# Four blocks of modulation rows beside the choice of keys, taken by GpSimd and a column of ones

## The chip, the cores and the metric

One NeuronCore of one Trainium2 chip runs the whole program in one launch. The metric is the device time of that launch in microseconds, lower is better. In the profile PE is TensorE's matmul, PEld its weight loads, DVE VectorE, ACT ScalarE, POOL GpSimd and SP the engine that issues the weight DMAs.

## The reference, cut to what matters

Three model blocks run one after the other over one sequence of 512 tokens with 1024 features, all in float32. The change lies in the first. There a modulation vector is made from a condition vector, two branches (RWKV and sparse attention) run on the same activations, and the branches are merged with sigmoid gates:

```python
mod = jax.nn.silu(c) @ w_ada + b_ada
shift, scale, gate = jnp.split(mod, 3, axis=-1)
h = rms_norm(x, norm_w) * (1.0 + scale[:, None, :]) + shift[:, None, :]
p = h @ w_in
...
idx_score = jnp.einsum('bqhs,bqh->bqs', jax.nn.relu(sc), iwb)
idx_score = jnp.where(adm[None], idx_score, -jnp.inf)
_, sel = lax.top_k(idx_score, topk)
...
yb = (yb * jax.nn.silu(gb)) @ w_b_out
merged = jax.nn.sigmoid(gm_a) * ya + jax.nn.sigmoid(gm_b) * yb
```

`top_k` takes 128 keys for each query: this is the choice of keys. The second model block has a modulation vector of its own (`w_mod`), which is needed only once the second block begins; its products with `silu(c_2)` are spread over the first block. A modulation vector is a product of one row (or of two, where a second condition is needed) with a 1024 x 512 weight block, so almost no arithmetic on 2 MB of weights.

## The kernel before

**Weights.** Weights are streamed from HBM in blocks of 2 MB (1024 rows by 512 columns, laid as 128 partitions by 8 by 512). In this part of the program they go into a ring of four slots, `weight_ring`. The order of the blocks is written out in `block1_plan`; `Chip.stream` (L223 to L265) issues them in that order from SP's queue, and before each issue SP waits until the last reader of the slot's former block has signalled (`free_at`). A block thus waits for the block four places ahead of it.

**Stages.** `project` (L493 on) runs one stage: a list of tiles in the order in which TensorE computes them. Each tile is (block, kind, place, source, tokens, evictions). A tile of kind "T" is 8 accumulated matmuls of 128x128 weights on 128x512 activations; one of kind "M" is a modulation tile; one of kind "X" is a transpose. ScalarE (first entry of the evictions) or VectorE (second) takes each finished tile out of PSUM. In this stage four PSUM banks are used in turn (`banks=4`), so that a tile waits for the eviction of the tile four places ahead. With `tensor_beside`, `scalar_beside` and `vector_beside` at -1, further work stands on an engine ahead of the tiles; `vector_after` stands behind them on VectorE.

**The stage of the change** is the sixth `project` of `block1`. It has seven blocks. Block 0 holds the gate columns of the attention branch (four tiles, `gates`), blocks 1 and 4 the sigmoid gates of the merge (four tiles each), blocks 2 and 3 the last two blocks of `w_ada`, and blocks 5 and 6 two blocks of `w_mod`. The stage's engines do this:

- TensorE first computes the 24 index dots of `dsa_scores` (L2130), three query groups of eight heads. ScalarE takes each through a ReLU (L2140) and VectorE multiplies it by its weight and adds it to the score (L2150 for the first head of a group, L2152 for the other seven, two inputs in SBUF). Four banks and four rooms lie between them: dot i waits for ReLU i-4, ReLU i waits for addition i-4.
- Then TensorE goes through the tiles, and VectorE, which evicts nothing here, makes the choice of keys, `dsa_select`: for each of three query groups an addition of the mask (L2170), 16 rounds of the eight largest (L2172) and their replacement (L2173), and the bias (L2174).
- An "M" tile (L617 to L620) loads the conditions `csil` (128 x 32) as weights and moves the weight block through the array in 32 matmuls of 128 columns. ScalarE copies the rows to `mstage` (L743); an "X" tile transposes them back to columns with one matmul (L592), and ScalarE adds the bias and writes `mod1` or `mod2` in four small operations (L736, `turn_beside_choice`).

The next stage is the attention (`dsa_attention`), whose first operation on VectorE (L2028) reads the bias that the choice of keys wrote. GpSimd has no work in this stage, nor anywhere ahead of the end of the second model block.

Of the kernel before, what the change touches and what calls it, by code (L numbers as in the profile page):

```python
# [16 lines left out]
ACT = mybir.ActivationFunctionType  # L17
AXX = mybir.AxisListType.X
MUL, ADD, SUB, MAX, MIN = ALU.mult, ALU.add, ALU.subtract, ALU.max, ALU.min

P = 128
T = 512
D = 1024
KD = D // P
# [467 lines left out]

def project(ch, nblocks, tiles, ahead=None, extra_sync=None, vector_first=None, vector_after=None, scalar_after=None,  # L493
            banks=BANKS, tensor_beside={}, vector_beside={}, scalar_beside={}, norm=None, normed_from=0, order=None, split=None,
            joined=None, early=None):

# [40 lines left out]
    with nullcontext(ch.block) as block:  # L539
        @block.sync  # L540
        def _(sp):
# [2 lines left out]
                extra_sync(sp)  # L544
            ch.stream(sp, first + nblocks + ahead)

        @block.tensor
        def _(pe):
            last = -1
            if joined:  # L550
                pe.wait_ge(by_act.sem, by_act.at(0))
                pe.wait_ge(by_dve.sem, by_dve.at(0))
            meet(pe)
            tensor_beside.get(-1, nothing)(pe)
            if split:
                count, half_ready, between = split
                ch.block_wait(pe, first)
                half_ready(pe)
                for n in range(count):
                    _, _, where, src, ntok, _ = tiles[n]  # L560
                    for k in range(2):
                        pe.matmul(ch.ps[:, order[n], 0:ntok], ch.block_view(first)[:, k, where:where + P], src[:, k, 0:ntok],
                                  start=k == 0, stop=False)
                    between.get(n, nothing)(pe)
            if early:
                count, half_ready, between = early
                for n in range(count):
                    b, _, where, src, ntok, _ = tiles[n]
                    ch.block_wait(pe, first + b)
                    for k in range(4):  # L570
                        half_ready(pe, k)
                        if k:
                            between.get(n - 1 + k / 4, nothing)(pe)
                        pe.matmul(ch.ps[:, order[n], 0:ntok], ch.block_view(first + b)[:, k, where:where + P], src[:, k, 0:ntok],
                                  start=k == 0, stop=False)
                    between.get(n, nothing)(pe)
            for n, t in enumerate(tiles):
                b, kind, where, src, ntok, ev = t
                i = first + b if b is not None else None
                if b is not None and b != last:  # L580
                    ch.block_wait(pe, i)
                    last = b
                if n >= R:
                    if tiles[n - R][5][1] is not None:
                        pe.wait_ge(by_dve.sem, by_dve.at(int(nv[n - R])))
                    else:
                        pe.wait_ge(by_act.sem, by_act.at(int(na[n - R])))
                m, f = shape(t)
                bank = ch.ps[:, order[n % R], :]
                if kind == "X":  # L590
                    pe.wait_ge(by_act.sem, by_act.at(int(na[where])))
                    ins = pe.transpose(bank[:, 0:P], src, ch.m("ident"))  # L592
                    ins.then_inc(ready.sem, 1)
                    ready.total += 1
                    tensor_beside.get(n, nothing)(pe)
                    continue
                w = ch.block_view(i)
                _, kt, c = ch.plan[i]
                if kind[0] == "W":
                    a_, b_, need_w, need_h = product_operands(ch, i, kind[1], src)  # L600
                    if need_w:
                        pe.wait_ge(weight_ready.sem, 4 * ch.sum_order[i] + need_w)
                    if (norm or src is not None) and need_h:
                        pe.wait_ge(h_ready.sem, h_ready.at(need_h))
                    for j in range(2):
                        if j == 1 and n - 0.5 in tensor_beside:
                            tensor_beside[n - 0.5](pe)
                        for k in range(4):
                            if n == normed_from and j == 0 and norm:
                                norm.wait(pe, k)  # L610
                            if n == normed_from + 1 and j == 0 and norm and kind[1] == 2:
                                norm.wait(pe, 4 + k)
                            cols = slice(j * P, (j + 1) * P)
                            st, mv = (b_[:, k, cols], a_[:, k, :]) if kind[2] else (a_[:, k, cols], b_[:, k, :])
                            ins = pe.matmul(bank[:, j * L:(j + 1) * L], st, mv, start=k == 0, stop=k == 3)  # L615
                elif kind == "M":
                    for k in range(kt):  # L617
                        for g in range(4):
                            ins = pe.matmul(bank[32 * g:32 * g + 32, 0:P], ch.csil[:, k, :],  # L619
                                            w[:, k, g * P:(g + 1) * P], start=k == 0, stop=k == kt - 1)  # L620
                else:
                    for k in range(2 if split and n < split[0] else 4 if early and n < early[0] else 0, kt):
                        if early and n == 0:
                            early[1](pe, k)
                        if n == normed_from and norm:
                            norm.wait(pe, k)
                        if k and n - 1 + k / kt in tensor_beside:
                            tensor_beside[n - 1 + k / kt](pe)
                        if kind == "T":
                            ins = pe.matmul(bank[0:m, 0:f], w[:, k, where:where + m], src[:, k, 0:ntok],  # L630
                                            start=k == 0, stop=k == kt - 1)
                        else:
                            c0 = kind[1] if isinstance(kind, tuple) else 0
                            ins = pe.matmul(bank[0:m, 0:f], src[:, k, where:where + P], w[:, k, c0:c0 + f],  # L634
                                            start=k == 0, stop=k == kt - 1)
                ins.then_inc(ready.sem, 1)
                ready.total += 1
                tensor_beside.get(n, nothing)(pe)
# [87 lines left out]
    return out + [turn_rows(ch, bands[x[0]], *x) for x in pending], len(place)  # L726


def turn_beside_choice(ch, band, i, m):

    dst, bias, first = band
    n = dst.shape[2]

    def part(a, act, ps, sig):
        for g in range(4):
            a(act.activation(dst[:, g, :], ps[:, 32 * g + first:32 * g + first + n], ACT.Identity, bias=bias[:, g:g + 1]),  # L736
              sig if g == 3 else None)
    return (None, "X", m, ch.mstage[:, i, :], T, (part, None))


def copy_to(out):

    return (lambda a, act, ps, sig: a(act.copy(out, ps), sig), None)  # L743


def act_to(out, func, **kw):
    return (lambda a, act, ps, sig: a(act.activation(out, ps, func, **kw), sig), None)
# [1451 lines left out]
def block1(ch):  # L2199
# [7 lines left out]

    gate, ga = ch.slot(3), ch.slot(5, 2)
    gates = [(0, "T", j * P, ch.hT, T, act_to(gate[:, j, :], ACT.Silu)) for j in range(4)]
    tiles = [(b, "T", j * P, ch.hT, T, act_to(ga[:, 4 * i + j, :], ACT.Sigmoid)) for i, b in enumerate((1, 4)) for j in range(4)]  # L2210
    bands = gate_bands(ch) + bands2(ch, 10, 12)
    rows = [(b, "M", 0, None, T, copy_to(ch.mstage[:, i, :])) for i, b in enumerate((2, 3, 5, 6))]
    turns = [turn_beside_choice(ch, band, i, m) for i, (band, m) in enumerate(zip(bands, (8, 9, 13, 15)))]
    tiles = (gates + tiles[0:4] + rows[0:2] + turns[0:1] + tiles[4:5] + turns[1:2] + rows[2:3] + tiles[5:6] + rows[3:4]
             + turns[2:3] + tiles[6:7] + turns[3:4] + tiles[7:8])
    project(ch, 7, tiles, banks=4, tensor_beside={-1: score_tensor}, scalar_beside={-1: score_scalar},
            vector_beside={-1: score_vector}, vector_after=dsa_select(ch))

    merged, gb, y, yb, tmp = ga, ch.slot(0, 2), ch.slot(2), ch.slot(11), ch.slot(9)
    tiles = []  # L2220
# [63 lines left out]
def block1_plan(A):  # L2284
# [4 lines left out]
    return ([ada[0], ada[1], lora, k, ada[2], ada[3], r, m[0], m[1], v, m[2], g, m[3], m[4], None, None]  # L2289
            + blocks(w, 3200, 3712) + blocks(w, 2176, 2688) + [None, None] + blocks(w, 2688, 3200)  # L2290
            + weave(blocks(w, 4224, 4736) + joined(w, [(4736, 4808)]), m[5:10]) + blocks(w, 3712, 4224)
            + blocks(w, 4808, 5320) + ada[4:6] + blocks(w, 5320, 5832) + m[10:12] + blocks(A["w_a_out"], 0, 1024)
            + blocks(w, 5832, 6856) + blocks(A["w_b_out"], 0, 1024)
            + blocks(A["w_o"], 0, 1024))

# [1511 lines left out]
```

## Time and profile before

| | us |
|---|---|
| median of 3 runs | 3161.09 |
| lowest and highest | 3160.84, 3163.19 |
| the profiled execution | 3161.36 |
| span of that execution in the trace | 3159.4 |

Of the span PE is busy 3015.5 us, VectorE 1552.0 us, ScalarE 700.8 us and GpSimd 9.6 us. The stage of the change starts at about 434.7 us of the span, with the index dots, and its last tile is evicted at 538.6 us.

How to read it: the rows below come from one profiled execution, and times in them count from the start of its span. In a timeline row the first number is the start, the second how long the stretch lasts; "xN" behind it is how many instructions of the same kind are merged in it, and the bracket holds idle time ahead of it and who ended it. One float32 matmul of the program is two matmul records in the trace, each with its own weight load; a transpose is one.

### The profile page before, as it was taken

How to read it: one execution, taken by the hardware profiler on the slowest of the kernel's cores; microseconds unless marked ns; L12 is line 12 of the kernel's file. 1: busy time of each engine (PE TensorE's matmuls, PEld its weight loads, DVE VectorE, ACT ScalarE, POOL GpSimd, SP SyncE). 2: the span in 40 equal slices, each digit the busy share in tenths (PEclk: the TensorE clock that was granted, in tenths of full speed). 3: DMA queues.
4: the chain of work that ended last, by engine and by line, in shares of the span. 5: the costliest groups of instructions: out<-in, count | busy, mean ns of one | idle time of the engine just before them, and what ended most of it. 6: DMA issues, size and time to landing. Idle time of an engine off the chain costs nothing.

```text
span 3159.4 us, 41395 instructions
## 1 busy us (share of the span) xinstructions
PE 3015.5 (95%) x17400; PEld 1797.4 (57%) x17400; DVE 1552.0 (49%) x2453; ACT 700.8 (22%) x1192; POOL 9.6 (0%) x10
## 2 busy tenths in 40 slices
PE   9999999999999899999899898999999999999998
PEld 4485544676457333332232233787588887887875
DVE  4463375655967322211211212545586857576663
ACT  4110332413063100000000001010632333331413
POOL 0000000000000000000000001000000000000000
PEclk9999999999999999999999999999999999999999
DMA  7301254031223899999999999131111211221210
GB/s 288 133 3 55 84 187 158 29 120 64 80 76 129 358 427 428 428 427 427 428 427 428 427 428 378 67 113 65 61 67 58 76 67 68 81 80 54 81 54 27
DMA packets 115575, 587.61 MB, mean 186 GB/s; under 512 B 6976, under 2 KB 8256, under 8 KB 89664
## 3 DMA queue, kind: packets, MB, share of 16 engines
q1 hardware_dynamic: 115392, 584.98, 46.2%
q8 instruction: 138, 2.26, 0.3%
q14 instruction: 45, 0.37, 0.0%
HBM read 582.86 MB, written 2.10 MB: 185 GB/s over the span
## 4 chain that ended last, share of the span: by engine, by line
PE 75%; DMA 15%; DVE 6%; issue 1%; SPq 1%; ACT 1%; DVEq 0%; ACTq 0%
PE ps L615 25%; PE ps L630 21%; DMA work<-in_w_up 7%; PE ps L2822 6%; DMA weight_ring<-in_w_up 5%; PE ps L2903 4%; PE ps L634 2%; PE ps L2785 2%; PE ps L1446 2%; DMA spare_slot<-in_w_up 1%; SPq L262 1%; PE ps L3535 1%; PE ps L3498 1%; PE ps L619 1%; DMA spare_slot<-in_first_weights 1%
## 5 line engine op out<-in xcount | busy, mean ns | idle before, releaser
L630 PE MATMUL ps<-hT,weight_ring 128*128 128x512 f32 (+1 forms) x1016 | 444.9, 594 | 1.4 <-ACT work L743 1.2
L630 PEld LDWEIGHTS ps<-hT,weight_ring 128*128 128x128 f32 (+1 forms) x1016 | 190.0, 190 | 233.3 <-issue 229.3
L399 DVE TENSOR_TENSOR work<-work,ps 128x512 f32<-128x512 f32 x203 | 139.5, 687 | 247.6 <-PE ps L615 243.5
L615 PE MATMUL ps<-weight_ring 128*128 128x256 f32 x992 | 225.6, 380 | 0.0
L2822 PE MATMUL ps<-work 128*64 128x512 f32 x832 | 191.0, 602 | 24.9 <-DMA work<-in_w_up 17.6
L630 PE MATMUL ps<-work,weight_ring 128*128 128x512 f32 (+1 forms) x496 | 210.6, 571 | 0.0
L2987 DVE SCALAR_TENSOR_TENSOR xT<-ps,mod,xT 128x512 f32<-128x512 f32 x128 | 96.1, 751 | 230.5 <-PE ps L2836 220.7
L2822 PE MATMUL ps<-weight_ring,work 128*64 128x512 f32 x800 | 181.7, 598 | 22.0 <-DMA weight_ring<-in_w_up 13.2
L615 PEld LDWEIGHTS ps<-weight_ring 128*128 128x128 f32 x992 | 187.1, 190 | 25.1
L615 PE MATMUL ps<-weight_ring,spare_slot 128*128 128x256 f32 x800 | 181.6, 380 | 0.0
L615 PE MATMUL ps<-hT,weight_ring 128*128 128x256 f32 x736 | 168.6, 386 | 6.3 <-DVE hT L850 3.8
L615 PEld LDWEIGHTS ps<-weight_ring,spare_slot 128*128 128x128 f32 x800 | 151.3, 190 | 20.8 <-issue 0.7
L615 PEld LDWEIGHTS ps<-hT,weight_ring 128*128 128x128 f32 x736 | 140.6, 193 | 27.9 <-issue 6.4
L2934 ACT ACTIVATE work<-ps 128x512 f32<-128x512 f32 x32 | 34.2, 1070 | 500.9 <-PE ps L2822 500.4
L2822 PEld LDWEIGHTS ps<-work 128*64 128x64 f32 x832 | 57.7, 137 | 150.8 <-issue 111.6
L630 PEld LDWEIGHTS ps<-work,weight_ring 128*128 128x128 f32 x496 | 90.8, 190 | 88.5 <-issue 84.4
L2822 PEld LDWEIGHTS ps<-weight_ring,work 128*64 128x64 f32 x800 | 55.3, 136 | 141.7 <-issue 107.3
L2981 DVE TENSOR_TENSOR work<-work,ps 128x512 f32<-128x512 f32 x32 | 33.9, 1058 | 188.8 <-PE ps L2822 188.3
L615 PE MATMUL ps<-work,weight_ring 128*128 128x256 f32 x448 | 100.9, 380 | 4.5 <-issue 4.5
L615 PEld LDWEIGHTS ps<-work,weight_ring 128*128 128x128 f32 x448 | 84.5, 190 | 16.8 <-issue 5.8
L2315 DVE SCALAR_TENSOR_TENSOR work<-work,vectors 128x512 f32<-128x512 f32 x120 | 90.2, 752 | 4.3
L2975 DVE TENSOR_TENSOR work<-ps,small 128x512 f32<-128x512 f32 (+1 forms) x17 | 11.2, 660 | 160.0 <-PE ps L2794 159.9
(490 smaller groups left out, 4150.0 us busy)
## 6 DMA issues: line engine op xcount, KB each, us to landing
work<-in_w_up SPq DMA_DIRECT2D x27, 2048.0 KB, 42.5
weight_ring<-in_w_gate SPq DMA_DIRECT2D x26, 2048.0 KB, 45.2
work<-in_w_gate SPq DMA_DIRECT2D x25, 2048.0 KB, 45.2
weight_ring<-in_w_down SPq DMA_DIRECT2D x24, 2048.0 KB, 44.5
weight_ring<-in_w_up SPq DMA_DIRECT2D x24, 2048.0 KB, 42.3
work<-in_w_down SPq DMA_DIRECT2D x24, 2048.0 KB, 44.9
weight_ring<-in_w_in_odd SPq DMA_DIRECT2D x20, 2048.0 KB, 7.7
weight_ring<-in_w_in SPq DMA_DIRECT2D x15, 2048.0 KB, 8.7
```

Of the source, the lines that this page charges most:

```text
L399: v(dve.tensor_tensor(out, x, got, op), sig if out is steps[-1][0] else None)
L615: ins = pe.matmul(bank[:, j * L:(j + 1) * L], st, mv, start=k == 0, stop=k == 3)
L630: ins = pe.matmul(bank[0:m, 0:f], w[:, k, where:where + m], src[:, k, 0:ntok], start=k == 0, stop=k == kt - 1)
L634: ins = pe.matmul(bank[0:m, 0:f], src[:, k, where:where + P], w[:, k, c0:c0 + f], start=k == 0, stop=k == kt - 1)
L1446: ins = pe.matmul(ps[rows, bank, cols], mat(left, par, q, s), moving, start=True, stop=True)
L2315: v(dve.scalar_tensor_tensor(y[:, j, :], src, tap, y[:, j, :], MUL, ADD), tapped if w == 30 else None)
L2785: ins = pe.matmul(ps[64 * q:64 * q + 64, bank, c], oh[:, s, :], hN[:, s, q * 512 + c.start:q * 512 + c.stop], start=s == 0, stop=s == 3)
L2822: ins = pe.matmul(ps[64 * h:64 * h + 64, 1 + 2 * u + n, :], xs[:, 2 * (i % 2) + t, i // 2, :], w[:, t, c0:c0 + 512], start=i == 0 and t == ...
L2903: ins = pe.matmul(ps[64 * q:64 * q + 64, 7, :], hidT[:, i // 2, t, i % 2, :], w[:, t, q * 512:(q + 1) * 512], start=i == 0 and t == 0, sto ...
L2934: a(act.activation(by_tile(hid[:, p, :]), strided(ps[:, 1 + p, :]), ACT.Silu), silus)
L2981: v(dve.tensor_tensor(by_tile(hid[:, p, :]), by_tile(hid[:, p, :]), strided(ps[:, 3 + p, :]), MUL), hid_ready)
L2987: v(dve.scalar_tensor_tensor(ch.xT[:, n, :], ps[:, scatter_banks(e, i // 2)[i % 2], :], ch.mod2[:, 40 + n, 0:1], ch.xT[:, n, :], MUL, ADD) ...
```

## The change

The modulation work of the four blocks moves from TensorE to GpSimd. For each of the four blocks GpSimd waits until it has arrived, multiplies it in place by the condition (`csil`, one column of the wanted condition, spread over 512), and adds its eight 512-wide pieces in three halving steps, the last into a room in work slot 1. It waits for each of its own four steps before the next, and counts them on `pool_step`. A new tile kind "C" has TensorE multiply the room with a column of ones: four matmuls of 128x128 weights on a 128x1 column, which sum over the partitions and leave 128 columns of modulation in one PSUM column each. The "M" tiles, the copies to `mstage` and the "X" tiles of this stage go. ScalarE's four small operations stay, on one column instead of one or two (the second condition's gate is not read).

The blocks of the stage stand in a new order in `block1_plan`: the `w_ada` blocks are now blocks 1 and 2, the first merge block is block 3, the `w_mod` blocks are 4 and 5, the second merge block is 6. A block that GpSimd reads is given back to SP by GpSimd's fourth step on it.

```diff
@@ project
-            joined=None, early=None):
+            joined=None, early=None, pool=None):
...
+        if pool:
+            block.gpsimd(pool)
...
+                if kind == "C":
+                    pe.wait_ge(*where)
+                    for g in range(4):
+                        ins = pe.matmul(bank[:, g:g + 1], src[:, g * P:(g + 1) * P], ch.m("ones")[:, 0:1], start=True, stop=True)
+                    ins.then_inc(ready.sem, 1)
+                    ready.total += 1
+                    tensor_beside.get(n, nothing)(pe)
+                    continue
...
-def turn_beside_choice(ch, band, i, m):
...
+def rows_on_pool(ch, first, rows):
+
+    rooms = ch.slot(1)
+    step = ch.counter("pool_step")
+    there = [(step.sem, step.at(4 * i + 4)) for i in range(len(rows))]
+    for i, (b, _) in enumerate(rows):
+        ch.free_at[first + b] = there[i]
+
+    def pool_rows(pool):
+        line = Line(pool, step)
+        ch.meet(pool)
+        for i, (b, (_, _, column)) in enumerate(rows):
+            ch.block_wait(pool, first + b)
+            w, acc = ch.block_view(first + b), rooms[:, i, :]
+            line(pool.tensor_tensor(w, w, ch.csil[:, :, column:column + 1].to_broadcast([P, KD, T]), MUL))
+            line(pool.tensor_tensor(w[:, 0:4, :], w[:, 0:4, :], w[:, 4:8, :], ADD))
+            line(pool.tensor_tensor(w[:, 0:2, :], w[:, 0:2, :], w[:, 2:4, :], ADD))
+            line(pool.tensor_tensor(acc, w[:, 0, :], w[:, 1, :], ADD))
+
+    def taken(i):
+        dst, bias, _ = rows[i][1]
+
+        def part(a, act, ps, sig):
+            for g in range(4):
+                a(act.activation(dst[:, g, 0:1], ps[:, g:g + 1], ACT.Identity, bias=bias[:, g:g + 1]), sig if g == 3 else None)
+        return (None, "C", there[i], rooms[:, i, :], T, (part, None))
+    return pool_rows, [taken(i) for i in range(len(rows))]
@@ block1
-    tiles = [(b, "T", j * P, ch.hT, T, act_to(ga[:, 4 * i + j, :], ACT.Sigmoid)) for i, b in enumerate((1, 4)) for j in range(4)]
+    tiles = [(b, "T", j * P, ch.hT, T, act_to(ga[:, 4 * i + j, :], ACT.Sigmoid)) for i, b in enumerate((3, 6)) for j in range(4)]
     bands = gate_bands(ch) + bands2(ch, 10, 12)
-    rows = [(b, "M", 0, None, T, copy_to(ch.mstage[:, i, :])) for i, b in enumerate((2, 3, 5, 6))]
-    turns = [turn_beside_choice(ch, band, i, m) for i, (band, m) in enumerate(zip(bands, (8, 9, 13, 15)))]
-    tiles = (gates + tiles[0:4] + rows[0:2] + turns[0:1] + tiles[4:5] + turns[1:2] + rows[2:3] + tiles[5:6] + rows[3:4]
-             + turns[2:3] + tiles[6:7] + turns[3:4] + tiles[7:8])
+    pool_rows, turns = rows_on_pool(ch, ch.used, list(zip((1, 2, 4, 5), bands)))
+    tiles = gates + tiles[0:3] + turns[0:2] + tiles[3:6] + turns[2:3] + tiles[6:7] + turns[3:4] + tiles[7:8]
     project(ch, 7, tiles, banks=4, tensor_beside={-1: score_tensor}, scalar_beside={-1: score_scalar},
-            vector_beside={-1: score_vector}, vector_after=dsa_select(ch))
+            vector_beside={-1: score_vector}, vector_after=dsa_select(ch), pool=pool_rows)
@@ block1_plan
-            + blocks(w, 4808, 5320) + ada[4:6] + blocks(w, 5320, 5832) + m[10:12] + blocks(A["w_a_out"], 0, 1024)
+            + ada[4:6] + blocks(w, 4808, 5320) + m[10:12] + blocks(w, 5320, 5832) + blocks(A["w_a_out"], 0, 1024)
```

TensorE's order in this stage before the change, from the index dots to the stage's end (numbers are the shape of the moving operand and how many instructions stand in a row):

```order
L2130 MATMUL ps<-work 128x512 x8
L630 MATMUL ps<-hT,weight_ring 128x512 x64
L619 MATMUL ps<-weight_ring,silu_of_conditions 32x128 x64
L592 MATMUL ps<-masks,modulation_rows 128x128
L630 MATMUL ps<-hT,weight_ring 128x512 x8
L592 MATMUL ps<-masks,modulation_rows 128x128
L619 MATMUL ps<-weight_ring,silu_of_conditions 32x128 x32
L630 MATMUL ps<-hT,weight_ring 128x512 x8
L619 MATMUL ps<-weight_ring,silu_of_conditions 32x128 x32
L592 MATMUL ps<-masks,modulation_rows 128x128
```

And the same place after the change, to the stage's end, where L641 is the old L630 and L596 the new tile:

```order
L2158 MATMUL ps<-work 128x512 x8
L641 MATMUL ps<-hT,weight_ring 128x512 x56
L596 MATMUL ps<-masks,work 128x1 x8
L641 MATMUL ps<-hT,weight_ring 128x512 x24
L596 MATMUL ps<-masks,work 128x1 x4
L641 MATMUL ps<-hT,weight_ring 128x512 x8
L596 MATMUL ps<-masks,work 128x1 x4
L641 MATMUL ps<-hT,weight_ring 128x512 x8
```

The 128 modulation matmuls and four transposes are gone, and 16 matmuls on one column stand behind the 7th, 10th and 11th of the 12 big tiles.

SP's queue at the same place before the change; the last three blocks ahead of the branch row are blocks 1 to 3 of the stage, and block 0 is the other one of the `x2`:

```order
L264 DMA weight_ring<-in_w_mod 128x8x512 x4
L264 DMA weight_ring<-in_w_in 128x8x512 x2
L264 DMA weight_ring<-in_w_ada 128x8x512 x2
L540 UNCONDITIONAL_BRANCH
L264 DMA weight_ring<-in_w_in 128x8x512
L264 DMA weight_ring<-in_w_mod 128x8x512 x2
L264 DMA weight_ring<-in_w_a_out 128x4x512 x2
```

SP's queue there after the change:

```order
L264 DMA weight_ring<-in_w_mod 128x8x512 x4
L264 DMA weight_ring<-in_w_in 128x8x512
L264 DMA weight_ring<-in_w_ada 128x8x512 x2
L264 DMA weight_ring<-in_w_in 128x8x512
L540 UNCONDITIONAL_BRANCH
L264 DMA weight_ring<-in_w_mod 128x8x512 x2
L264 DMA weight_ring<-in_w_in 128x8x512
L264 DMA weight_ring<-in_w_a_out 128x4x512 x2
```

The `w_ada` blocks moved one place forward, and the second merge block went from ahead of the two `w_mod` blocks to behind them; the amount of data is the same.

## Rows read from the trace of the kernel before

**Rows 1.** The page: busy time of each engine; granted PE clock in 40 slices.

```profile
PE 3015.5 (95%) x17400; PEld 1797.4 (57%) x17400; DVE 1552.0 (49%) x2453; ACT 700.8 (22%) x1192; POOL 9.6 (0%) x10
...
PEclk9999999999999999999999999999999999999999
```

**Rows 2.** The chain that ended last, 430 to 545 us: start, us, what.

```profile
435.97 11.00 PE ps L2130 x35
446.97 55.13 PE ps L630 x128
502.11 3.63 PE ps L619 x128
505.74 0.26 PE ps L592
505.99 6.87 PE ps L630 x16
512.97 1.88 PE ps L619 x64
...
531.04 6.88 PE ps L630 x16
538.01 0.61 ACT work L747
538.66 0.49 PE ps L1969 x4
```

**Rows 3.** Timeline of DVE, end of the choice and start of the attention.

```profile
513.15 0.43 DVE L2174 TENSOR_SCALAR work<-work 128x512 f32<-128x512 f32 x1
539.34 0.29 DVE L2028 CUSTOM_DVE_ANT_0 work<-ps,work 128x128 f32<-128x128 f32 x1 [25.77 <-PE ps L1969]
```

**Rows 4.** L2634 and L2649: records, ns min/median/max, first and last start in us.

```profile
L2634 PE MATMUL ps<-masks,work x8: 262/262/263, 1023.5 to 1024.3; 128*128 128x16 f32 x8
...
L2649 PE MATMUL ps<-small,masks x32: 200/201/228, 1028.0 to 1029.2; 128*32 128x4 f32 x32
```

**Rows 5.** Timeline of SP's queue, 426 to 429 us, and DMAs issued there with us to landing.

```profile
426.97 0.89 SPq L264 DMA_DIRECT2D weight_ring<-in_w_in  x1
...
weight_ring<-in_w_in SPq DMA_DIRECT2D x1, 2048.0 KB, 15.3
```

**Rows 6.** The same two views, 429 to 431 us and 474 to 475.5 us.

```profile
weight_ring<-in_w_ada SPq DMA_DIRECT2D x1, 2048.0 KB, 18.0
...
474.73 0.37 SPq L264 DMA_DIRECT2D weight_ring<-in_w_in  x1
...
weight_ring<-in_w_in SPq DMA_DIRECT2D x1, 2048.0 KB, 7.6
```

**Rows 7.** Groups by line and form: GpSimd's one operation, and VectorE's two-input sums.

```profile
L3018 POOL TENSOR_SCALAR work<-xT,small 128x512 f32<-128x512 f32 x6 | 9.4, 1582 | 1957.2 <-DVE xT L2987 1957.2
...
L3591 DVE TENSOR_TENSOR work<-work 128x2048 f32<-128x2048 f32 x8 | 18.3, 2292 | 0.3
...
L3464 DVE TENSOR_TENSOR work<-work 128x512 f32<-128x512 f32 x32 | 22.1, 691 | 1.1
```

**Rows 8.** Timeline of DVE, 436 to 452 us: the score additions.

```profile
440.54 4.54 DVE L2152 SCALAR_TENSOR_TENSOR work<-work,small 128x384 f32<-128x384 f32 x7
445.12 0.49 DVE L2150 TENSOR_SCALAR work<-work,small 128x512 f32<-128x512 f32 x1
445.64 5.48 DVE L2152 SCALAR_TENSOR_TENSOR work<-work,small 128x512 f32<-128x512 f32 x7
```

**Rows 9.** GpSimd and VectorE side by side: L3018 and L3010, ns min/median/max; timeline at 1965 us.

```profile
L3018 POOL TENSOR_SCALAR work<-xT,small x6: 1562/1563/1677, 1957.3 to 1965.3; 128x512 f32<-128x512 f32 x6
...
L3010 DVE TENSOR_SCALAR work<-xT,small x2: 486/596/706, 1966.1 to 1966.6; 128x512 f32<-128x512 f32 x2
...
1965.35 1.68 POOL L3018 TENSOR_SCALAR work<-xT,small 128x512 f32<-128x512 f32 x1
1966.08 0.49 DVE L3010 TENSOR_SCALAR work<-xT,small 128x512 f32<-128x512 f32 x1
```

More of the change, by code:

```diff
@@ L726, in modulated @@
     return out + [turn_rows(ch, bands[x[0]], *x) for x in pending], len(place)
-def turn_beside_choice(ch, band, i, m):
[L731 to L738, printed above, removed]
+def rows_on_pool(ch, first, rows):
[21 more added lines that the diff above has]
+    return pool_rows, [taken(i) for i in range(len(rows))]
 def copy_to(out):
```

## The prediction

> **What bounds the kernel now.** I read the page's busy line first, then the chain that ended last, cut to this stage, then VectorE's timeline, to see whether TensorE or the choice of keys ends the stage. PE is busy 95% of the span at a full granted clock [rows 1]: the level of 2.4 GHz, with no fall near this stage. In the chain the stage is TensorE from the index dots to the last tile: 11.0 us of dots to 446.97, eight big tiles in 55.13 us (6.89 each), then modulation and four more tiles to 538.01, where ScalarE's last eviction hands over to the attention at 538.66 [rows 2]. VectorE ends the choice at 513.58 and does nothing until 539.34, when it waits for TensorE [rows 3]. So TensorE's time is the stage's time, the choice has 25.8 us to spare, and GpSimd is empty. A saving here is not given back later for any reason that I see: the later transfers are issued when TensorE frees their slots, and shift with it.
>
> **What TensorE loses.** From 502.11 to 538.01 there are 35.90 us, in which four big tiles take 6.87 to 6.88 each, 27.5 in all [rows 2]. The rest, 8.4 us, is modulation: two blocks at once cost 3.63, the other two 1.88 each (one of them in the rows), 7.4 together, and about 1.0 is four transposes and the gaps at their ends. All of it lies on the path. Taken away: **-8.4**.
>
> **What TensorE gains.** Sixteen matmuls of full 128x128 weights on one column are 32 records. The nearest row has the same weights on 16 columns: eight records start between 1023.5 and 1024.3, seven steps of 0.114 us [rows 4]. The weight load sets this pace and doesn't shrink with the column, so 32 x 0.114 = 3.65 us. Bounds: records with 32 weight columns start 31 steps in 1.2 us, 0.039 each, giving 1.2 us; with nothing overlapped the record's own 262 ns would give 8.4 us [rows 4]. I take 3.65, since weights and shape are the same there. In the old order a tile behind a modulation block cost up to 0.2 us more, so three places add about 0.3. **+3.95**. The net is -4.45, and the tiles would end at 533.6 if TensorE waits for nothing.
>
> **ScalarE** loses four copies and keeps its sixteen small operations. It was waiting for TensorE; nothing on the path. The banks are no tighter: two C tiles in a row need banks whose tiles were evicted long before.
>
> **When GpSimd can start.** The first `w_ada` block takes the place in SP's queue that the merge block had: issued at 426.97, landed 15.3 us later, at 442.3 [rows 5]. The second one takes the next place, issued at 429.68 and landed 18.0 later, at 447.7 [rows 6]. Its other wait, for the engines of the stage before, ends ahead of that, near 434.6. The merge block now comes third, near 452, and is wanted only behind four tiles at 474.5. The first `w_mod` block waits for block 0's last tile as the merge block did: issued at 474.73, landed 482.3 [rows 6]. The second is issued at once behind it if GpSimd is done with block 1, and lands near 488.
>
> **How fast GpSimd is.** It does 4096 + 2048 + 1024 + 512 = 7680 columns for a block. The trace has it only in L3018, one input, 512 columns in 1562 ns: 3.05 ns a column [rows 7, 9], so 23.4 us a block. The lower bound is VectorE with two inputs, 2292 ns for 2048 or 1.12 a column, 8.6 us a block [rows 7]. Part of L3018 is the start of an instruction: VectorE's two-input sum falls from 1.35 ns a column at 512 to 1.12 at 2048, a factor of 0.83 [rows 7]. The same factor on 3.05 gives 2.53 ns and **19.4 us a block**, which I take: it is the row of this engine, corrected for length. That a second input costs more isn't in any row; it is in the range. The Trainium skill, "GPSIMD Engine Reference", section "Performance versus the Vector engine", has 4497 ns for a two-input float32 sum of 2048 columns, which by estimate would make about 17 us a block and change nothing below.
>
> **What waits for GpSimd.** TensorE is queued in order, so each C tile that comes too early holds every tile behind it. Times in the new order: tiles 1 to 7 end at 495.2, then blocks 1 and 2 are wanted, and come at 442.3 + 38.8 = 481. The second merge block needs the slot of block 2: issued at 481, landed about 489 to 494, wanted at 504 behind one more tile. Block 4 is wanted at 517.8: it starts at 482.3 (landing) and is done by 502. Block 5 is wanted at 525.7 and done at 521. Nothing waits, but the last C tile has only 4 us of slack. The general rule: with T us a block, block 5 is done at 442.3 + 4T, so **T = 21** (2.7 ns a column) is the point from which TensorE waits, and each us of T more costs 4.
>
> **VectorE beside GpSimd.** From 442.3 on GpSimd reads SBUF beside the score additions. The only overlap in the trace: the first L3010 ran from 1966.08 in 486 ns wholly inside a GpSimd operation that lasted to 1967.03 and wasn't slowed, the second took 706, and GpSimd's own 1677 instead of 1562 [rows 9]. So a slowing of up to 1.45, and no standstill. The additions that TensorE's last dot hangs on are those of the 384-wide group; they end at 445.08, and the last four start after 442.3, 0.65 us each [rows 8]. At 1.45 that is 4 x 0.29 = **+1.1** on TensorE (bounds: 0 from the unslowed one, and the standstill below). The eight 512-wide additions and the small operations of the choice may be slowed too, but have the 25.8 us to hide in; the rounds of L2172 and L2173 read one tensor.
>
> **Sum.** Against the profiled execution: 3161.4 - 8.4 + 3.95 + 1.1 = 3158.0. The profiled execution is 0.3 above the median, which is well within its error: I forecast **3158.0**.
>
> **Rival 1, GpSimd as slow as its row.** At 23.4 us a block, block 5 is done at 442.3 + 93.7 = 536.0. TensorE waits from 526.8 to 536.0 and ends at 536.0 + 1.0 + 6.9 = 543.9, 5.9 later than now: **3167**. For it: it is the only row of this engine, and has one input where the change has two. Against: the length of the instructions. It decides from 21 us a block, breaks even at 22.
>
> **Rival 2, a standstill.** If a two-input VectorE operation had to wait for the whole of a GpSimd instruction that is under way, the last four 384-wide additions would each sit out one of the four steps of block 1 (19.4 us together), then the next four ones those of block 2. TensorE's dots end 19.4 later and the tiles at 553. The choice starts 39 later and meets the steps of blocks 4 and 5 at its mask additions and bias operations, some 11 more, to end at 564; the attention then starts about 25 late instead of TensorE's 15. That is 3176 to 3187, say **3182**, slower. Against it speaks the unslowed L3010 inside L3018 [rows 9], which has one tensor input; for it, that no row has two inputs beside GpSimd. The Trainium skill, "SBUF — State Buffer", section "Who interferes with whom", states just this: a shared port pair as an exclusive lock for a whole instruction, taken also by a VectorE operation with two SBUF inputs. By the row on L3010 the trace doesn't agree for one input; for two it is silent.
>
> **Rival 3, it moves nothing.** If the small matmuls cost their full 262 ns a record, the 8.4 us come back whole: **3161.5**. The steps of 0.114 speak against it.
>
> **How the numbers follow.** A measurement of this kernel can tell about 0.2% from no change, 6.3 us, so 3154.8 to 3167.4 is "same". The forecast with its own range 3155.5 to 3160.5: 0.60. Rival 1: 0.16, over 3160 to 3172, half of it inside "same". Rival 2: 0.16. Rival 3: 0.08. The saving can pass 6.3 only if the column matmuls run at 0.039 a record (8.4 - 1.2 - 0.3 = 6.9 without contention): 0.05 of the first case. Faster 0.05, same 0.55 + 0.08 + 0.08 = 0.71, slower 0.08 + 0.16 = 0.24. The range 3155 to 3170 holds the forecast's case, rival 3 and most of rival 1, 0.80.
>
> **What would show it.** No L619 and L592 in this stage, and 32 records of L596 in about 3.7 us. GpSimd's four steps of a block at about 10.4, 5.2, 2.6 and 1.3 us; the last block's end before TensorE wants it, and L596 with no idle time ahead of it. The 384-wide additions at up to 0.9 us instead of 0.65, and the first big tile at 447 to 448.5. If a two-input addition shows 5 to 10 us, rival 2 holds; if L596 waits for POOL at 526, rival 1. The forecast is wrong too if the second merge block lands after 504, or if the choice ends behind TensorE.

## The result and the profile after

The changed kernel takes 3176.24 us (median of 4 runs, 3175.13 to 3177.98) against 3160.97 us for the kernel before: a ratio of 1.0047, 95% interval 1.0035 to 1.0059. It is 15 us slower, where I forecast 3158.0 within 3155 to 3170. Its profiled execution took 3175.13 us, with a span of 3173.2. Line numbers of the changed kernel differ: L2158 is the dot, L2168 the ReLU, L2178 and L2180 the score additions, L2198, L2200, L2201 and L2202 the mask addition, the rounds and the bias of the choice, L641 the big tile, L754 to L757 GpSimd's four steps.

The timeline of TensorE over the stage (start, length, work, idle before and by whom), to be read against [rows 2]:

```profile
434.64 10.26 PE L2158 MATMUL ps<-work 64*128 64x256 f32 x42 [0.42 <-DVE mod L710]
451.26 2.07 PE L2158 MATMUL ps<-work 64*128 64x512 f32 x2 [6.36 <-ACT work L2168]
456.03 2.07 PE L2158 MATMUL ps<-work 64*128 64x512 f32 x2 [2.70 <-ACT work L2168]
458.65 2.07 PE L2158 MATMUL ps<-work 64*128 64x512 f32 x2 [0.55 <-ACT work L2168]
460.65 50.60 PE L641 MATMUL ps<-hT,weight_ring 128*128 128x512 f32 x112
511.09 1.84 PE L596 MATMUL ps<-masks,work 128*128 128x1 f32 x16
512.79 20.85 PE L641 MATMUL ps<-hT,weight_ring 128*128 128x512 f32 x48
...
542.04 7.11 PE L641 MATMUL ps<-hT,weight_ring 128*128 128x512 f32 x16
550.80 0.49 PE L1997 MATMUL ps<-work 64*128 64x128 f32 x4 [1.64 <-DVE work L2202]
```

The dots end 13.7 us later than in [rows 2], where the first big tile started at 446.97. The last three come in steps of several microseconds, and each waits for ScalarE's ReLU, which waits for VectorE. The timelines of GpSimd and of VectorE show why. GpSimd:

```profile
443.05 7.03 POOL L754 TENSOR_TENSOR weight_ring<-weight_ring,silu_of_conditions 128x4096 f32<-128x4096 f32 x1 [442.63 <-DMA weight_ring<-in_w_ada]
450.16 4.69 POOL L755 TENSOR_TENSOR weight_ring<-weight_ring 128x2048 f32<-128x2048 f32 x1
454.93 2.54 POOL L756 TENSOR_TENSOR weight_ring<-weight_ring 128x1024 f32<-128x1024 f32 x1
457.54 1.46 POOL L757 TENSOR_TENSOR work<-weight_ring 128x512 f32<-128x512 f32 x1
459.08 7.09 POOL L754 TENSOR_TENSOR weight_ring<-weight_ring,silu_of_conditions 128x4096 f32<-128x4096 f32 x1
```

VectorE beside it, single operations. Before the change seven 384-wide additions took 4.54 us together [rows 8], 0.62 us each and small gaps:

```profile
443.05 7.45 DVE L2180 SCALAR_TENSOR_TENSOR work<-work,small 128x384 f32<-128x384 f32 x1
450.53 4.73 DVE L2180 SCALAR_TENSOR_TENSOR work<-work,small 128x384 f32<-128x384 f32 x1
455.30 2.58 DVE L2180 SCALAR_TENSOR_TENSOR work<-work,small 128x384 f32<-128x384 f32 x1
457.92 1.37 DVE L2178 TENSOR_SCALAR work<-work,small 128x512 f32<-128x512 f32 x1
459.32 7.40 DVE L2180 SCALAR_TENSOR_TENSOR work<-work,small 128x512 f32<-128x512 f32 x1
```

Each operation takes about as long as the GpSimd step beside it, 7.0, 4.7, 2.5, 1.5, 7.1, and ends a few tenths after it. Between two steps exactly one gets in. That is the standstill of rival 2. The last dot hangs on the last 384-wide addition, so three operations stood on TensorE's path: 7.45 + 4.73 + 2.58 us instead of 3 x 0.62, which is 12.9 us more.

Two more costs stand in the views. The granted clock, in the table of stretches (us, busy time and count of PE, PEld, DVE, ACT and POOL, then PEclk, DMA share, GB/s):

```profile
434.00:447.00 13.00, 10.39 (x43) 5.79 (x43) 10.77 (x15) 7.58 (x17) 3.95 (x1) 1.00 1.05 386
447.00:466.00 19.00, 11.49 (x13) 3.81 (x14) 18.86 (x5) 2.39 (x4) 18.69 (x5) 0.55 0.24 89
466.00:503.00 37.00, 37.00 (x88) 16.41 (x87) 35.10 (x78) 7.34 (x10) 13.62 (x5) 1.00 0.31 112
```

TensorE was idle from 444.9 to 451.3, and the clock then stood at the lower of its two levels, 1.2 GHz, for most of the second stretch, into the first big tile. The first seven big tiles take 50.60 us instead of 48.33 in the experiments below where the clock didn't fall: 2.3 us. The last dot takes 2.07 us where e2 below has 1.12 for it, 0.95 more. So the clock costs 3.2 us in all. And the choice of keys, from VectorE's timeline:

```profile
515.45 5.95 DVE L2202 TENSOR_SCALAR work<-work 128x384 f32<-128x384 f32 x1
521.44 4.48 DVE L2198 TENSOR_TENSOR work<-work,masks 128x128 f32<-128x128 f32 x1
550.23 0.43 DVE L2202 TENSOR_SCALAR work<-work 128x512 f32<-128x512 f32 x1
```

It ends at 550.66 instead of 513.58 [rows 3], 37 us later (27.4 us from the score additions, 9.8 from the slowed operations L2202 and L2198), which uses up the 25.8 us that it had to spare: the attention's first matmul waits for it (`DVE work L2202`, last line of TensorE's timeline). The rounds in between, L2200 and L2201, are not slowed at all: on 384 columns, where GpSimd works beside most of them, they take 561 and 543 ns on average in both kernels.

The account of the stage, from the first dot to the attention's first matmul: 103.9 us before (434.75 to 538.66), 116.2 after (434.64 to 550.80). Of the +12.3, the dots give +13.9 (12.9 of standing additions and 0.95 of the clock in the last dot), the clock in the tiles +2.3, the choice that is last +0.9; TensorE's saving takes 4.8 off. The attention starts 12.1 us later in the span than before, and the span grew by 13.8, so 1.7 us arose behind the stage; the medians differ by 15.3. The cause of that part stays open.

### The profile page after: what moved, and what is told of

The parts are those of the page before. It is cut to its first block, busy times and chain, and to the rows that moved or that the text cites. A ratio compares the mean times of both kernels' runs of the same rounds, so it can differ in the third digit from the quotient of the medians.

```text
span 3173.2 us, 40948 instructions
## 1 busy us (share of the span) xinstructions
PE 3017.4 (95%) x17172; PEld 1795.6 (57%) x17172; DVE 1589.3 (50%) x2453; ACT 699.7 (22%) x1188; POOL 71.9 (2%) x26
## 4 chain that ended last, share of the span: by engine, by line
PE 70%; DMA 17%; DVE 9%; issue 1%; ACT 1%; SPq 1%; DVEq 0%; ACTq 0%
PE ps L626 25%; PE ps L641 18%; PE ps L2848 6%; DMA weight_ring<-in_w_up 6%; DMA work<-in_w_up 4%; PE ps L2929 3%; DMA weight_ring<-in_w_gate 3%; PE ps L645 2%; DMA weight_ring<-in_w_down 2%; PE ps L1474 2%; PE ps L2811 1%; DMA spare_slot<-in_w_up 1%; SPq L262 1%; DVE work L2180 1%; DVE work L2201 1%
## 5 line engine op out<-in xcount | busy, mean ns | idle before, releaser
L641 PE MATMUL ps<-hT,weight_ring 128*128 128x512 f32 (+1 forms) x1016 | 447.1, 596 | 1.4 <-ACT work L771 1.2
L641 PEld LDWEIGHTS ps<-hT,weight_ring 128*128 128x128 f32 (+1 forms) x1016 | 190.6, 190 | 235.6 <-issue 231.6
L641 PE MATMUL ps<-work,weight_ring 128*128 128x512 f32 (+1 forms) x496 | 210.5, 570 | 0.0
L641 PEld LDWEIGHTS ps<-work,weight_ring 128*128 128x128 f32 x496 | 90.8, 190 | 88.6 <-issue 84.5
```

## The experiments

Each is an edit of the changed kernel. "The stage" is always the time from the first dot to the attention's first matmul.

**e1_late: GpSimd starts after the score additions.**

```diff
         ch.meet(pool)
+        masked = ch.S["first_masked"]
+        pool.wait_ge(masked.sem, masked.at(1))
...
-            v(dve.tensor_tensor(row[:, n - P:n], row[:, n - P:n], ch.m("adm"), ADD))
+            v(dve.tensor_tensor(row[:, n - P:n], row[:, n - P:n], ch.m("adm"), ADD), masked if s == 1 else None)
```

> The changed kernel with one wait more: GpSimd starts its first multiplication only when VectorE has done the first mask addition of the choice of keys (about 452 us), so that no score addition runs beside it. Theory A (a VectorE operation that needs the port it shares with GpSimd stands until GpSimd's whole instruction is over): the dots end at 447 as before the change, TensorE's tiles at 533.6, no fall of the clock; the choice's mask additions and bias operations still wait about 5 us each for GpSimd's steps, 20 us in all, and end near 535, so 3157 us (3156 to 3159), faster than both kernels. Theory B (the new tiles or the new order of the blocks cost the time, GpSimd's neighbourhood little): it stays at 3170 to 3177.

Measured: 3159.19 us against 3161.97 of the kernel before on the same chip, ratio 0.9991 (0.9983 to 1.0000), just above the 3156 to 3159 that I expected. The stage takes 100.3 us (436.25 to 536.56). Its timelines of TensorE, and of VectorE in the choice:

```profile
436.25 12.22 PE L2160 MATMUL ps<-work 64*128 64x256 f32 x48 [0.42 <-DVE mod L710]
448.41 48.33 PE L641 MATMUL ps<-hT,weight_ring 128*128 128x512 f32 x112
...
536.56 0.49 PE L1999 MATMUL ps<-work 64*128 64x128 f32 x4 [1.91 <-DVE work L2205]
```

```profile
468.99 7.14 DVE L2205 TENSOR_SCALAR work<-work 128x256 f32<-128x256 f32 x1
476.17 4.55 DVE L2201 TENSOR_TENSOR work<-work,masks 128x128 f32<-128x128 f32 x1
...
500.75 6.42 DVE L2205 TENSOR_SCALAR work<-work 128x384 f32<-128x384 f32 x1
507.20 4.48 DVE L2201 TENSOR_TENSOR work<-work,masks 128x128 f32<-128x128 f32 x1
```

The dots run in 12.2 us again, and the whole loss is gone with nothing changed but GpSimd's start. Theory B, that the new tiles or the new order of the blocks cost the time, falls. As expected the four operations of the choice still wait, 21.3 us together, and the choice is last by 1.2 us: the attention's first matmul waits 1.91 us, for L2205, where 0.75 for ScalarE is the rule.

**e2_early_pieces: the same work, started early, in pieces of 512 columns.**

```diff
...
-            line(pool.tensor_tensor(w, w, ch.csil[:, :, column:column + 1].to_broadcast([P, KD, T]), MUL))
-            line(pool.tensor_tensor(w[:, 0:4, :], w[:, 0:4, :], w[:, 4:8, :], ADD))
-            line(pool.tensor_tensor(w[:, 0:2, :], w[:, 0:2, :], w[:, 2:4, :], ADD))
+            for k in range(0, 8, 1):
+                line(pool.tensor_tensor(w[:, k:k + 1, :], w[:, k:k + 1, :],
+                                        ch.csil[:, k:k + 1, column:column + 1].to_broadcast([P, 1, T]), MUL))
+            for half in (4, 2):
+                for k in range(0, half, 1):
+                    line(pool.tensor_tensor(w[:, k:k + 1, :], w[:, k:k + 1, :], w[:, half + k:half + k + 1, :], ADD))
...
```

> The changed kernel with GpSimd's work cut into pieces of 512 columns (15 instructions for a block instead of 4), started early as in the change. Theory A: each of the four 384-wide additions that TensorE's dots hang on waits for at most one piece of about 1 us instead of 7.0, 4.7, 2.5 and 1.5: the dots end at 449 to 451.5 instead of 460.7, the clock doesn't fall, and the time is 3160 to 3162. Theory C (GpSimd slows VectorE in proportion to how long both run, whatever the length of an instruction): the additions take as long as in the change, 3174 to 3178.

Measured: 3162.17 us against the same 3161.97, ratio 1.0002 (0.9993 to 1.0011), just above the expected 3160 to 3162. One addition and the piece beside it, from the two timelines, and the last dot with the tiles behind it:

```profile
443.12 1.28 DVE L2183 SCALAR_TENSOR_TENSOR work<-work,small 128x384 f32<-128x384 f32 x1
...
442.73 1.25 POOL L755 TENSOR_TENSOR weight_ring<-weight_ring,silu_of_conditions 128x512 f32<-128x512 f32 x1 [442.31 <-DMA weight_ring<-in_w_ada]
...
447.79 1.12 PE L2161 MATMUL ps<-work 64*128 64x512 f32 x2 [0.19 <-ACT work L2171]
448.84 48.33 PE L641 MATMUL ps<-hT,weight_ring 128*128 128x512 f32 x112
```

The additions take 1.28 us beside pieces of 1.25, and no longer 7.45. The first big tile starts 2.0 us late instead of 13.9, and the stage takes 101.1 us. GpSimd does the same sums, and is busy with them for longer: the first block takes 21.4 us instead of 16.0. Only the length of an instruction changed. Theory C, a slowing in proportion to the time side by side, falls: what counts is how long the instruction is that an operation of VectorE happens to meet.

**e3_tiny: GpSimd's sums left out.** The blocks aren't multiplied and summed; four sums of 8 columns keep the order of waits.

```diff
-            line(pool.tensor_tensor(w, w, ch.csil[:, :, column:column + 1].to_broadcast([P, KD, T]), MUL))
-            line(pool.tensor_tensor(w[:, 0:4, :], w[:, 0:4, :], w[:, 4:8, :], ADD))
-            line(pool.tensor_tensor(w[:, 0:2, :], w[:, 0:2, :], w[:, 2:4, :], ADD))
-            line(pool.tensor_tensor(acc, w[:, 0, :], w[:, 1, :], ADD))
+            for _ in range(4):
+                line(pool.tensor_tensor(acc[:, 0:8], w[:, 0, 0:8], w[:, 1, 0:8], ADD))
```

> The changed kernel with GpSimd's four steps of a block cut to 8 columns each: the products and sums of the four modulation blocks are left out, while waits, order of the blocks and the sixteen column matmuls stay. Theory A and C: what TensorE saves by itself, 4.4 us: 3156.6 (3156 to 3157.5). Theory B: 3170 or more.

Measured: 3158.80 us against 3161.97, ratio 0.9989 (0.9980 to 0.9998); the profiled execution took 3157.0. The first dot and the attention's first matmul:

```profile
434.71 12.23 PE L2156 MATMUL ps<-work 64*128 64x256 f32 x48 [0.42 <-DVE mod L710]
...
533.85 0.49 PE L1995 MATMUL ps<-work 64*128 64x128 f32 x4 [0.75 <-ACT work L773]
```

The stage takes 99.1 us, 4.8 less than before the change. This is the effect of the new tiles and of the new block order with next to nothing beside them, and it is a gain of the size forecast. The median saves 3.2 us rather than 4.4 and lies above the expected 3156 to 3157.5, so my bound for it was too sharp.

**e4_late_pieces: the late start, and pieces of 1024 columns.** The edits of e1 and e2 together, with steps of 2 in place of 1.

> The late start of e1, with GpSimd's work in pieces of 1024 columns (the last of a block 512). Theory A: the mask additions and bias operations wait at most 2.3 us each, so the choice ends before 525, well ahead of TensorE: 3156.6 (3156 to 3158), at or a little below e1. Theory C: like e1, with the same total delay of the choice in both.

Measured: 3159.13 us against 3161.97, ratio 0.9989 (0.9981 to 0.9998); profiled 3157.44. The median lies above the expected 3156 to 3158. The stage takes 99.1 us, the same as with GpSimd's sums left out:

```profile
436.22 12.22 PE L2163 MATMUL ps<-work 64*128 64x256 f32 x48 [0.42 <-DVE mod L710]
...
535.36 0.49 PE L2002 MATMUL ps<-work 64*128 64x128 f32 x4 [0.75 <-ACT work L780]
```

The choice in VectorE's timeline:

```profile
468.95 1.08 DVE L2208 TENSOR_SCALAR work<-work 128x256 f32<-128x256 f32 x1
470.07 1.94 DVE L2204 TENSOR_TENSOR work<-work,masks 128x128 f32<-128x128 f32 x1
...
518.78 1.04 DVE L2208 TENSOR_SCALAR work<-work 128x512 f32<-128x512 f32 x1
```

It ends at 519.8, far ahead of TensorE's last tile. This version is faster than both kernels, over the one before by 0.11% with an interval that only just leaves out zero: a small gain. Between e1 and e4 the medians show no difference; the stage does, 1.2 us.

**e5_memsets: GpSimd writes and reads nothing.** Each of the four steps is a `memset` of the same columns; the products and sums are left out.

```diff
-            line(pool.tensor_tensor(w, w, ch.csil[:, :, column:column + 1].to_broadcast([P, KD, T]), MUL))
+            line(pool.memset(w, 1.0))
...
```

> The changed kernel, started early as in the change, but each of GpSimd's sixteen steps only writes a constant over the same columns (4096, 2048, 1024, 512): the products and sums are left out, and GpSimd reads nothing. It is to tell which side of the shared port holds VectorE up. Theory A1 (VectorE's second input needs a read path that GpSimd's reads hold): the two-input additions beside it keep their 0.62 and 0.75 us, the dots end at 447. Theory A2 (any GpSimd instruction on SBUF holds up such an addition): the additions beside the first two blocks wait for whole steps, and one takes as long as the longest step. If the steps are too short to see (under 1 us), A1 and A2 are told apart by whether any addition is above 0.8 us.

Measured: 3158.25 us in its one run, against 3162.53 in one run of the kernel before on the same chip; the stage takes 99.1 us. GpSimd's first two memsets, then VectorE's operations beside them and beside later ones:

```profile
443.01 3.51 POOL L754 MEMSET weight_ring<- 128x4096 f32 x1 [442.58 <-DMA weight_ring<-in_w_ada]
446.58 1.97 POOL L755 MEMSET weight_ring<- 128x2048 f32 x1
...
490.48 3.51 POOL L754 MEMSET weight_ring<- 128x4096 f32 x1
```

```profile
441.14 4.54 DVE L2180 SCALAR_TENSOR_TENSOR work<-work,small 128x384 f32<-128x384 f32 x7
445.72 1.08 DVE L2178 TENSOR_SCALAR work<-work,small 128x512 f32<-128x512 f32 x1
446.83 5.48 DVE L2180 SCALAR_TENSOR_TENSOR work<-work,small 128x512 f32<-128x512 f32 x7
...
490.54 3.67 DVE L2202 TENSOR_SCALAR work<-work 128x384 f32<-128x384 f32 x1
```

The fourteen two-input additions take what they took before the change, 4.54 and 5.48 us in all [rows 8], beside memsets of up to 3.5 us. So it is GpSimd's reading that stops a two-input addition: A1, not A2. But the one-input operations L2178 and L2202 do wait, 1.08 instead of 0.49 us [rows 8] and 3.67 instead of 0.36, until the memset beside them is over, and so does the copy L2194, 1.44 instead of 0.23. Since a memset only writes, they must need something that GpSimd's writing holds.

**e6_one_input: GpSimd's steps with one input.** Each is a product with a scalar of its partition, in the form of L3018; the sums are left out.

```diff
-            line(pool.tensor_tensor(w, w, ch.csil[:, :, column:column + 1].to_broadcast([P, KD, T]), MUL))
+            one = ch.csil[:, 0, column:column + 1]
+            line(pool.tensor_scalar(w, w, one, None, MUL))
...
```

> The changed kernel, started early, with each of GpSimd's steps a multiplication of one input by a scalar of its partition (the form of L3018 in the kernel before) over the same columns: the sums are left out. Theory A1: GpSimd still reads, so a two-input addition beside it waits for the whole step; if a step takes 3 ns a column as L3018 did, the first addition takes some 12 us and the dots end after 460. Theory D (what I read from L3018 and L3010, that a one-input GpSimd operation doesn't stop VectorE, or only for a small part of it): the additions stay under 1.1 us and the dots end before 449.

Measured: 3169.15 us in its one run, against the same 3162.53; the stage takes 109.8 us, and the first big tile starts at 457.78. GpSimd's step, and VectorE's timeline from the addition that met it (two instructions merged, of which only the first was held up) to the one that met the next step:

```profile
444.00 10.63 POOL L755 TENSOR_SCALAR weight_ring<-weight_ring,silu_of_conditions 128x4096 f32<-128x4096 f32 x1 [443.58 <-DMA weight_ring<-in_w_ada]
454.72 5.72 POOL L756 TENSOR_SCALAR weight_ring<-weight_ring,silu_of_conditions 128x2048 f32<-128x2048 f32 x1
```

```profile
444.07 9.88 DVE L2181 SCALAR_TENSOR_TENSOR work<-work,small 128x384 f32<-128x384 f32 x2
454.00 0.62 DVE L2181 SCALAR_TENSOR_TENSOR work<-work,small 128x384 f32<-128x384 f32 x1
...
455.17 4.08 DVE L2181 SCALAR_TENSOR_TENSOR work<-work,small 128x512 f32<-128x512 f32 x1
```

Theory D falls for long steps: one input or two, an addition stands. But not to the step's end. The merged pair is 9.23, 0.03 and 0.62 us, so the first of them took its 0.62 us from about 452.7 on, and two more ran inside the step, which ended at 454.63. The next stood until 459.25 - 0.75 = 458.50, while its step ended at 460.44. In both cases VectorE got in 1.9 us before the end, which is why the dots ended before the 460 that I expected of theory A1.

Beside the step of 512 columns, the length of L3018, an addition waits only 0.3 us, 1.06 instead of 0.75. But a one-input operation of VectorE, the form of L3010, waits for the end of a long step:

```profile
463.63 1.72 POOL L758 TENSOR_SCALAR work<-weight_ring,silu_of_conditions 128x512 f32<-128x512 f32 x1
463.96 1.06 DVE L2181 SCALAR_TENSOR_TENSOR work<-work,small 128x512 f32<-128x512 f32 x1
...
494.40 10.63 POOL L755 TENSOR_SCALAR weight_ring<-weight_ring,silu_of_conditions 128x4096 f32<-128x4096 f32 x1 [8.09 <-DMA weight_ring<-in_w_mod]
503.10 2.14 DVE L2203 TENSOR_SCALAR work<-work 128x384 f32<-128x384 f32 x1
```

L2203 takes 2.14 us instead of 0.36 and ends at 505.24, 0.2 us after the step.

## Why the prediction was wrong, point by point

- **TensorE's part was right.** I forecast -8.4 and +3.95; the new tile stands in the trace at 0.95 us for 8 records and 1.84 for 16, of which 0.8 and 1.7 lie on the path, and the stage of e3 saves 4.8 us against the forecast 4.45. Rival 3 is out.
- **When GpSimd starts was right**: 442.3 forecast, 443.05 measured.
- **GpSimd's speed was on the safe side.** I took 19.4 us a block; it is 15.4 undisturbed (e1: 7.03, 4.53, 2.35, 1.26 and the gaps), and 16.0 and 16.4 in the change's first two. That is 1.72 ns a column for the product with a column spread out, 2.2 for a true two-input sum. L3018's 3.05 doesn't carry over to another form. Rival 1 is out. The Trainium skill, "GPSIMD Engine Reference", "Performance versus the Vector engine", has 4497 ns for a two-input sum of 2048 columns, and the trace agrees with 4.5 us (e1).
- **The step that failed is "VectorE beside GpSimd".** I read [rows 9] as a slowing of at most 1.45 and applied it to the additions: +1.1 us. They cost +12.9, and the last dot another 0.95 at the lower clock. The row was one short GpSimd instruction with one input, beside a VectorE operation with one input, and the additions have two. The second L3010, at 706 instead of 486 ns, did show a wait: it ended 0.3 us after L3018, which was over at 1967.03, so its own 0.49 us of work can have begun 0.2 us before that end and not from its start. I took the ratio of the two instead of asking what the second had waited for.
- **Why the first L3010 ran free stays open.** It began 0.73 us into L3018. In e6 the addition beside a step of the same form and length got its 0.75 us of work from 0.64 us into the step on, so GpSimd's reading may have been over by then; but L2203, a one-input operation, waited for the end of its step, and no run has one beside so short a step. Nor was this the only overlap in the trace, as I wrote: the additions L2987 ran beside L3018 too and kept their 0.75 us, but one of their two inputs lies in PSUM.
- **Rival 2 was the mechanism**: 384-wide operations against the steps of block 1, one let in between two steps. Its span of 3176 to 3187 holds the result, at its lower edge. Its price of 19.4 us for the dots was too high for two reasons: GpSimd's block takes 16.0, and three additions stood, not four, since GpSimd started 0.75 us later than I assumed; the fourth to stand was the one-input L2178, which the dots don't wait for. That makes 12.9. I put the choice at 564, and it ended at 550.66: the additions delayed it by 27.4 us instead of 39, while the mask additions and bias operations gave 9.8 for my 11. What I left out is the clock's fall in the idle stretch, 3.2 us with the last dot.
- **The page that I set against the row was right.** The Trainium skill, "SBUF — State Buffer", "Who interferes with whom", says that a VectorE operation with two SBUF inputs is held up by a GpSimd one that reads SBUF and not by one that only writes, and that the lock lasts for the whole instruction. The trace agrees on the first two (7.45 us beside the product, 0.62 beside the memset). On the third it agrees for two-input steps, to some 0.2 us, and not for one-input ones, which let an addition in 1.9 us early. The page also names `tensor_scalar` and copies, when in a two-port mode, as operations that can take the shared pair, which fits L2178, L2202 and L2194 beside memsets. I gave this 0.16, on the strength of one overlap that didn't have the form in question.

## What to carry to other kernels

Before work is put on GpSimd, list VectorE's operations in that stretch by form: those with two SBUF inputs, and short scalar or copy operations between SBUF tensors, may stand for the whole of a GpSimd instruction; the search rounds with one tensor don't. If some of them are on the path of another engine, start GpSimd behind them, or cut its work into short pieces: pieces of 1.25 us left 2.0 of the 13.9 us. A row that shows two engines side by side speaks only for its own forms and lengths; where the two don't match the change, the bound is the longest instruction, and it belongs in the range.

## What the runs showed of the hardware that I hadn't expected

- A two-input addition of VectorE took 7.45, 4.73 and 2.58 us beside GpSimd steps of 7.03, 4.69 and 2.54, and 1.28 beside pieces of 1.25, for the same 0.62 us of work.
- GpSimd's own cost is small: its steps grew from 7.03, 4.53, 2.35 and 1.26 us (e1) to 7.03, 4.69, 2.54 and 1.46 when an addition slipped in between each two.
- With a one-input GpSimd operation, the two-input addition got in 1.9 us before that operation's end, at 2048 columns as at 4096 (e6). A one-input operation of VectorE didn't, and waited for the end.
- Cutting a block's 4 instructions into 8, pieces of 1024 columns, costs GpSimd little: 16.5 us a block instead of 15.4 (e4). Cut into 15, pieces of 512, it is 18.3 (e2, block 4).
